# A two-block transformer on one core: the last block's bias rows made and stored during the third feed-forward part, and its scaled latents, their squares and rotation terms kept in PSUM

## The reference, cut to what matters

```python
# first block: h = h + 0.5*swiglu(..); a mixer (a scan in layer 0, sparse attention in layer 1); h = h + 0.5*swiglu(..)
# so there are four feed-forward parts, f0, f1, f2, f3; f3 is the last step of the first block
# second block:
xn = rms_norm_2(h, norm_mix_g)
qa, ka, va, c_q, c_kv, k_rope = split(xn @ w_in)        # widths 512 512 512 768 256 32
out_a = dilated_attention(rms(qa), rms(ka), va, rel_bias)     # 8 heads, logits + bias by distance
qb = rms_norm_2(c_q, cq_norm_g) @ w_uq                  # 8 heads of 96
kv = rms_norm_2(c_kv, ckv_norm_g) @ w_ukv               # 8 heads of 64 (key) + 64 (value)
qb, kb = rms_norm_2(qb, g), rms_norm_2([k_nope, k_rope for every head], g)
qb, kb = rotary embedding on the last 32 of 96 columns of each
out_b = causal_attention(qb, kb, vb)
h = h + concat(out_a, out_b) @ w_o
h = h + square(relu(rms_norm_2(h, norm_ffn_g) @ w_ff1)) @ w_ff2
```

## Time and profile before

| | us |
|---|---|
| median of 3 runs | 1781.03 (1777.22 to 1782.37) |
| the profiled execution, whole | 1785.45 |
| its span, first to last instruction | 1783.4 |
| TensorE busy, share of the span | 1612.4, 90% |
| GpSimd busy | 1097.2, 62% |
| VectorE busy | 801.8, 45% |
| ScalarE busy | 739.8, 41% |

### The profile page before, as it was taken

The page is one execution under the profiler, slowest core; times in us unless marked ns, Lnnn a source line. Parts: engine busy times, 40 slices in busy tenths (PEclk is TensorE's granted clock), DMA queues, the critical chain, the costliest instruction groups (busy, mean ns, idle before and its releaser), DMA issues.

```text
span 1783.4 us, 40019 instructions
## 1 busy us (share of the span) xinstructions
PE 1612.4 (90%) x15940; PEld 1522.0 (85%) x15940; DVE 801.8 (45%) x1576; ACT 739.8 (41%) x1204; POOL 1097.2 (62%) x552
## 2 busy tenths in 40 slices
PE   6999979659888899999999997999989969869998
PEld 6999979438886799999999985699989957769998
DVE  4332374684435733343334477663345635453300
ACT  4444434512312344444444432644435434544532
POOL 5778857343301578787787763068868753328896
PEclk9999989768767899999999997999999988889999
DMA  6454533100010344455444542035436632214552
GB/s 228 165 180 147 195 115 138 43 1 2 3 49 25 119 159 171 144 186 189 166 172 150 198 144 95 1 129 186 172 126 203 185 126 95 95 48 165 188 192 91
DMA packets 38777, 231.27 MB, mean 130 GB/s; under 512 B 4511, under 2 KB 7680, under 8 KB 17552
## 3 DMA queue, kind: packets, MB, share of 16 engines
q1 hardware_dynamic: 34560, 225.49, 35.9%
q10 hardware_dynamic: 4112, 4.31, 1.1%
HBM read 227.09 MB, written 2.62 MB: 129 GB/s over the span
## 4 chain that ended last, share of the span: by engine, by line
PE 77%; DVE 11%; issue 7%; POOL 3%; ACT 1%; DMA 0%; SPq 0%; DVEq 0%; ACTq 0%; POOLq 0%
PE PS L737 62%; POOL wlo L691 3%; PE PS L736 1%; DVE xl L1618 1%; DVE xg L1702 1%; DVE ss L1632 1%; PE PS L915 1%; PE PS L930 1%; PE PS L954 1%; PE PS L922 1%; DVE score L2038 1%; PE PS L960 1%; PE PS L1284 1%; ACT whi L2395 1%; DVE prnb L2316 1%
## 5 line engine op out<-in xcount | busy, mean ns | idle before, releaser
L691 POOL TENSOR_TENSOR wlo<-raw,whi 128x1024 fp32r<-128x1024 f32 (+1 forms) x472 | 1036.1, 2217 | 579.7 <-ACT whi L2395 530.2
L737 PE MATMUL PS<-xh,whi 128*128 128x272 f32 (+1 forms) x2336 | 689.5, 295 | 79.1 <-POOL wlo L691 35.9
L737 PE MATMUL PS<-xl,whi 128*128 128x272 f32 (+1 forms) x2336 | 678.5, 290 | 0.0
L737 PE MATMUL PS<-xh,wlo 128*128 128x272 f32 (+1 forms) x2336 | 677.3, 290 | 0.0
L2395 ACT ACTIVATE whi<-raw 128x1024 fp32r<-128x1024 f32 (+1 forms) x472 | 447.5, 980 | 260.0 <-PE PS L737 205.9
L737 PEld LDWEIGHTS PS<-xh,whi 128*128 128x128 f32 x2336 | 451.1, 193 | 93.4 <-issue 35.9
L737 PEld LDWEIGHTS PS<-xl,whi 128*128 128x128 f32 x2336 | 452.7, 194 | 0.6
L737 PEld LDWEIGHTS PS<-xh,wlo 128*128 128x128 f32 x2336 | 452.4, 194 | 0.0
L737 PE MATMUL PS<-hid_h,whi 128*128 128x272 f32 (+1 forms) x960 | 274.9, 286 | 12.1 <-POOL wlo L691 11.9
L737 PE MATMUL PS<-hid_h,wlo 128*128 128x272 f32 (+1 forms) x960 | 274.4, 286 | 0.0
L737 PE MATMUL PS<-hid_l,whi 128*128 128x272 f32 (+1 forms) x960 | 273.6, 285 | 0.0
(11 more groups left out here) (382 smaller groups left out, 1771.8 us busy)
## 6 DMA issues: line engine op xcount, KB each, us to landing
raw<-w_f_in_in SPq DMA_DIRECT2D x88, 1024.0 KB, 4.8
raw<-w_f_dn_in SPq DMA_DIRECT2D x64, 704.0 KB, 4.0
raw<-w_b_ff_in SPq DMA_DIRECT2D x32, 1024.0 KB, 4.8
raw<-w_rk_r_in SPq DMA_DIRECT2D x4, 1024.0 KB, 4.8
raw<-w_rk_k_in SPq DMA_DIRECT2D x4, 1024.0 KB, 4.7
raw<-w_rk_v_in SPq DMA_DIRECT2D x4, 1024.0 KB, 4.8
raw<-w_rk_o_in SPq DMA_DIRECT2D x4, 1024.0 KB, 4.9
raw<-w_at_q_in SPq DMA_DIRECT2D x4, 1024.0 KB, 5.0
```

What stands on the lines that cost most here:

```text
L691: nc.gpsimd.tensor_tensor(wlo[U % SPL][:, part], raw[U % RAW][:, part], whi[U % SPL][:, part].bitcast(F32), ALU.subtract).then_inc(s_lo, 1)
L737: mm(out, a, b, start=start and n == 0, stop=stop and n == 2, **kw)
```

## The change

1. The product of the bias rows moves from the head of the last block to the start of `f3_dn`, into the second bank of that stage's first group. VectorE's copy to `biasw` moves from after the normalization to right after the angle tables. ACT's store moves from behind `latent(0)` to right behind the two sines, ahead of `residual("f3_dn")`, whose first job is `hi` of unit 2.
2. The wait for the store and the eight bias loads move from behind the square of `kr` (just ahead of `hi(b_ka)`) to just ahead of `hi(b_cq+2)`.
3. The scaled latents (`cxf`) are now in PSUM banks 2 and 3, and their squares `csq` in bank 5.
4. `kg` is made from PSUM in one instruction instead of from `kr`; the key's product with the sine stays in PSUM bank 3, the queries' in bank 2; `qg` is made from PSUM before `qr` is drained, and its two instructions become one.

```diff
             def swiglu(f):
                 project(f + "_in", tok[f], 0, f, norm=f)
+                if f == "f3":
+                    G = G0["f3_dn"]
+                    pe.wait_ge(s_free, G - 1)
+                    pe.wait_ge(s_bc, 112)
+                    mm(PS[0:8, bank(G) + 1, 0:384], relb[:, :], distt[:, :], start=True, stop=True).then_inc(s_bwm, 1)
...
-            pe.wait_ge(s_bc, 112)
-            mm(PS[0:8, 4, 0:384], relb[:, :], distt[:, :], start=True, stop=True).then_inc(s_bwm, 1)
...
-            pe.wait_ge(b_kg, 1)
+            pe.wait_ge(s_free, G0["b_tail"] + 1)
             mm(PS[:, 3, 0:SEQ], rot_b[:, :], kg[:, :], start=True, stop=True).then_inc(s_hrot, 1)
...
+            dve.wait_ge(s_bwm, 1)
+            v.tensor_copy(biasw[:, :], PS[0:8, bank(G0["f3_dn"]) + 1, 0:384]).then_inc(s_bw, 1)
             residual("f3_dn", SEQ, 1, 2, 0.5, "b", VEC["norm_mix"], "b")
             rms("b", SEQ)
-            dve.wait_ge(s_bwm, 1)
-            v.tensor_copy(biasw[:, :], PS[0:8, 4, 0:384]).then_inc(s_bw, 1)
...
-                step.do(v.tensor_scalar(cxf[:, u % 2, 0, :], craw[:, u % 2, 0, :], col(VEC["cq_g"] + 2 * u), None, ALU.mult))
+                step.do(v.tensor_scalar(scaled_latent(u)[:, 0, :], craw[:, u % 2, 0, :], col(VEC["cq_g"] + 2 * u), None, ALU.mult))
...
-            v.tensor_tensor(kr[:, :], PS[:, G % 2, 0:SEQ], rstd[:, 0:SEQ], ALU.mult).then_inc(s_free, 1)
-            dve.wait_ge(s_free, G + 1)
-            v.tensor_scalar(kg[:, :], kr[:, :], col(VEC["kb_r"]), None, ALU.mult).then_inc(b_kg, 1)
+            step.do(v.tensor_tensor(kr[:, :], PS[:, G % 2, 0:SEQ], rstd[:, 0:SEQ], ALU.mult))
+            v.scalar_tensor_tensor(kg[:, :], PS[:, G % 2, 0:SEQ], col(VEC["kb_r"]), rstd[:, 0:SEQ], ALU.mult,
+                                   ALU.mult).then_inc(s_free, 1)
...
-            v.tensor_tensor(rtt[:, 0, :], PS[:, 3, 0:SEQ], cs_b[:, 1, :], ALU.mult).then_inc(b_rotd, 1)
+            step.do(v.tensor_tensor(PS[:, 3, 0:SEQ], PS[:, 3, 0:SEQ], cs_b[:, 1, :], ALU.mult))
             step(v.tensor_tensor(krot[:, :], kg[:, :], cs_b[:, 0, :], ALU.mult))
-            dve.wait_ge(b_rotd, 1)
-            step(v.tensor_tensor(krot[:, :], krot[:, :], rtt[:, 0, :], ALU.add))
+            v.tensor_tensor(krot[:, :], krot[:, :], PS[:, 3, 0:SEQ], ALU.add).then_inc(b_rotd, 1)
...
                 if J == 3:
+                    G = G0["b_uq"]
+                    dve.wait_ge(s_unit, 2 * (U0["b_uq"] + 1))
+                    v.tensor_scalar(qg[:, :, :], chunk_pair(G), col(VEC["qb_r"]), None, ALU.mult).then_inc(b_qg, 1)
                     queries_drain(0, qr[:, :, :])
-                    dve.wait_ge(s_free, G0["b_uq"] + 1)
-                    for q in range(2):
-                        v.tensor_scalar(qg[:, q, :], qr[:, q, :], col(VEC["qb_r"]), None, ALU.mult).then_inc(b_qg, 1)
...
@@ ACT
             for n in range(2):
                 act.wait_ge(s_ang, n + 1)
                 f(cs_b[:, n, :], cs_b[:, n, :], ACT.Sin).then_inc(s_sin, 1)
+            act.wait_ge(s_bw, 1)
+            act.dma_start(t["rows"].rearrange("(p h x) -> h p x", p=128, h=8),
+                          biasw[:, :].unsqueeze(1).broadcast_to([8, 128, 384])).then_inc(s_bst, 16)
             residual("f3_dn", SEQ, 1, 2, "b", "b")
...
             hi(U0["b_cq"] + 1)
             root("b", SEQ)
+            act.wait_ge(s_bst, 16)
+            pitch = 8 * 384 - 1
+            skewed = t["rows"][127:127 + 128 * pitch].rearrange("(p w) -> p w", w=pitch)
+            for hd in range(8):
+                act.dma_start(bias[:, hd, :], skewed[:, hd * 384:hd * 384 + 256]).then_inc(s_bld, 16)
             hi(U0["b_cq"] + 2)
             latent(0)
-            act.wait_ge(s_bw, 1)
-            act.dma_start(t["rows"].rearrange("(p h x) -> h p x", p=128, h=8),
-                          biasw[:, :].unsqueeze(1).broadcast_to([8, 128, 384])).then_inc(s_bst, 16)
             hi(U0["b_ckv"])
...
             f(krs[:, :], kr[0:32, :], ACT.Square).then_inc(b_sqk, 1)
-            act.wait_ge(s_bst, 16)
-            act.wait_ge(s_bst, 16)
...
-            for hd in range(8):
-                act.dma_start(bias[:, hd, :], skewed[:, hd * 384:hd * 384 + 256]).then_inc(s_bld, 16)
             hi(U0["b_ka"])
```

More of the change, by code:

```diff
@@ L411, in build @@
         craw = b2("craw", [128, 2, 2, SEQ])
-        cxf = b2("cxf", [128, 2, 2, SEQ])
-        csq = b2("csq", [128, 2, SEQ])
         squares = Region(rings)("squares", [128, 8, SEQ])
+        b2.here = rings + 4 * 8 * SEQ
         kr = b2("kr", [128, SEQ])
@@ L426, in build @@
         vbt = b2("vbt", [128, 2, 512])
-        rtt = b2("rtt", [128, 2, SEQ])
         hinva = b2("hinva", [16, SEQ])
@@ L551, in build @@
         b_sqk, b_sqq, b_sumk, b_sumq = sem("k_squared"), sem("q_squared"), sem("k_summed"), sem("q_summed")
-        b_kg, b_qg, b_rotd, b_f, b_om = (sem("k_rope_gain"), sem("q_rope_gain"), sem("rope_added"), sem("query_factor"),
+        b_qg, b_rotd, b_f, b_om = (sem("q_rope_gain"), sem("rope_added"), sem("query_factor"),
                                          sem("output_product"))
@@ L712, in build, with scaled_latent @@
         AT2, AT5 = 2, 5
+        def scaled_latent(g):
+            return PS[:, 2 + g % 2, :].rearrange("p (q n) -> p q n", q=2)
+        csq = PS[:, 5, :].rearrange("p (q n) -> p q n", q=2)
         def chunk_pair(G):
@@ L1549, in _ @@
             b_queries(1, 1)
-            pe.wait_ge(b_qg, 2)
+            pe.wait_ge(b_qg, 1)
             pe.wait_ge(s_hsc, AT5 + 7)
@@ L1569, in _ @@
             last.then_inc(b_sumq, 1)
-            pe.wait_ge(b_rotd, 3)
+            pe.wait_ge(b_rotd, 2)
             scores(8)
@@ L2184, in latent_low @@
                 dve.wait_ge(s_xh, X0["cq"] + g + 1)
-                low(latl[:, 2 * g:2 * g + 2, :], cxf[:, g % 2, :, :], lath[:, 2 * g:2 * g + 2, :], s_x)
+                low(latl[:, 2 * g:2 * g + 2, :], scaled_latent(g), lath[:, 2 * g:2 * g + 2, :], s_x)
             for u in range(4):
@@ L2194, in _ @@
                     dve.wait_ge(s_xh, X0["cq"] + u - 1)
-                step.do(v.tensor_scalar(cxf[:, u % 2, 0, :], craw[:, u % 2, 0, :], col(VEC["cq_g"] + 2 * u), None, ALU.mult))
-                v.tensor_scalar(cxf[:, u % 2, 1, :], craw[:, u % 2, 1, :], col(VEC["cq_g"] + 2 * u + 1), None,
+                step.do(v.tensor_scalar(scaled_latent(u)[:, 0, :], craw[:, u % 2, 0, :], col(VEC["cq_g"] + 2 * u), None, ALU.mult))
+                v.tensor_scalar(scaled_latent(u)[:, 1, :], craw[:, u % 2, 1, :], col(VEC["cq_g"] + 2 * u + 1), None,
                                 ALU.mult).then_inc(s_xm, 1)
@@ L2203, in _ @@
                         dve.wait_ge(s_css, 1)
-                    v.tensor_tensor(bt[0][:, :, :], bt[0][:, :, :], csq[:, :, :], ALU.add).then_inc(s_css, 1)
+                    v.tensor_tensor(bt[0][:, :, :], bt[0][:, :, :], csq, ALU.add).then_inc(s_css, 1)
             U, G = U0["b_tail"], G0["b_tail"]
@@ L2271, in _ @@
             dve.wait_ge(s_hb, AT5 + 5)
+            dve.wait_ge(b_rotd, 1)
             v.tensor_tensor(krf[:, :, :], krot[:, :].unsqueeze(1).broadcast_to([128, 2, SEQ]), spread_pair(2),
@@ L2350, in _ @@
                     dve.wait_ge(s_hrot, AT5 + 2)
-                    v.tensor_tensor(rtt[:, :, :], spread_pair(2), sin, ALU.mult).then_inc(b_rotd, 1)
+                    step.do(v.tensor_tensor(spread_pair(2), spread_pair(2), sin, ALU.mult))
                     dve.wait_ge(b_sqq, 1)
                     step(v.tensor_tensor(qr[:, :, :], qg[:, :, :], cos, ALU.mult))
-                    dve.wait_ge(b_rotd, 2)
-                    v.tensor_tensor(qr[:, :, :], qr[:, :, :], rtt[:, :, :], ALU.add).then_inc(b_rotd, 1)
+                    v.tensor_tensor(qr[:, :, :], qr[:, :, :], spread_pair(2), ALU.add).then_inc(b_rotd, 1)
                 if J == 7:
@@ L2682, in latent @@
                     act.wait_ge(s_css, 1)
-                f((bt[0], csq, csq, bt[1])[g][:, :, :], craw[:, g % 2, :, :], ACT.Square).then_inc(s_csq, 1)
+                f((bt[0][:, :, :], csq, csq, bt[1][:, :, :])[g], craw[:, g % 2, :, :], ACT.Square).then_inc(s_csq, 1)
                 act.wait_ge(s_xm, XM0["cq"] + g + 1)
-                f(lath[:, 2 * g:2 * g + 2, :], cxf[:, g % 2, :, :], ACT.Copy).then_inc(s_xh, 1)
+                f(lath[:, 2 * g:2 * g + 2, :], scaled_latent(g), ACT.Copy).then_inc(s_xh, 1)
             def heads_square(name, u, j):
@@ L2706, in _ @@
             f(krs[:, :], kr[0:32, :], ACT.Square).then_inc(b_sqk, 1)
-            act.wait_ge(s_bst, 16)
-            pitch = 8 * 384 - 1
-            skewed = t["rows"][127:127 + 128 * pitch].rearrange("(p w) -> p w", w=pitch)
-            for hd in range(8):
-                act.dma_start(bias[:, hd, :], skewed[:, hd * 384:hd * 384 + 256]).then_inc(s_bld, 16)
             hi(U0["b_ka"])
```

## The result

Over eight runs each, the changed kernel took 1772.08 us (1764.18 to 1777.35) and the kernel before 1781.57 (1775.86 to 1786.62): ratio 0.994, 95% interval 0.9915 to 0.9966, that is 6 to 15 us faster. (A ratio is always the time of a kernel divided by that of the kernel before.) The profiled execution took 1777.35, its span 1775.5. The forecast was 1769.2, range 1760 to 1779, and -11.8 as a difference; measured is -9.5.

The account below looks back on a forecast made before the run. Bound: TensorE's products plus holes, mainly its wait behind ScalarE's store. Terms -18.0 - 1.2 - 0.1 - 0.8 + 0.4 + 0.6 + 7.3 = -11.8, from the median 1781.0 to 1769.2 us; range 1760 to 1779.

Parts of the forecast that it names:

- Store out of the last block: Last block, before `b_ka`: TensorE's 15.1 us hole closes, and the slow first unit's 2.9 us with it; gain 18.0.
- VectorE's shorter path: Last block: scaled latents in PSUM shorten VectorE's path to `csq`, for which ScalarE and TensorE waited; gain 1.2.
- +0.4 for the loads: Bias loads ahead of `hi(b_cq+2)` hold ScalarE 3.7 us, delaying that unit's copy; cost 0.1 to 0.5, say 0.4.
- -0.1: Last block's head: the bias product and copy go away; gain 0 to 0.7, taken as 0.1.
- The head of f3_dn: Start of `f3_dn`: the copy to `biasw` and the store's issue delay `whi` of unit 2; cost 0.6.
- The store beside the loads: `f3_dn`: the store delays unit 6's load, giving TensorE a 5.6 us hole plus 1.7 restart; cost 7.3.
- The hidden store: Rival, `f3_dn`: unit 6's load waits only some 17 packets, landing at 1337.5, no hole; -19.1, 1762; chance 0.20.
- The second wait: Rival, last block: a slip of `b_ka` or `b_ukv` takes part of the gain, leaving -6, 1775; chance 0.16.
- The store that holds its engines to its end: Rival, `f3_dn`: unit 6 lands only with the store's end, hole 20.8 us; +4.6, 1786; chance 0.12.
- Operands in PSUM at J = 3: Attention step J = 3: `qg` takes about 0.8 instead of 2.75 us; gain 0 to 1.9, taken as 0.8.
- the probabilities meet the same POOL work: Attention step J = 3: probabilities behind the earlier logits still meet POOL's work, so the gain could be 0; no chance given.

Follow-up runs that it names:

- bias_only: Kernel before with only the bias product, copy, store and loads in their new places, all operands as they were: 1773.1 us, ratio 0.9946.
- copies32_late: Changed kernel with bias rows stored 32 times instead of 128, and bias product, copy, store and loads in their old places: 1765.0 us, ratio 0.9904.
- before_copies32: Kernel before with one edit, bias rows stored 32 times instead of 128 and loads of 32 partitions by four heads: 1765.6 us, ratio 0.9921.
- loads_back: Changed kernel with the wait and the eight bias loads back behind the square of `kr`: 1762.3 us in one execution.
- psum_only: Changed kernel with everything of the bias back in its old place, so only the operands in PSUM remain: 1783.3 us, ratio 1.000.
- copies64: Changed kernel with bias rows stored 64 times instead of 128, two heads to a load: 1764.9 us in one execution.
- copies32: Changed kernel with bias rows stored 32 times instead of 128, each load filling 32 partitions for four heads: 1763.9 us, ratio 0.990.
- after: The changed kernel itself, against the kernel before: 1772.08 us, ratio 0.994.
- after_again: The changed kernel measured once more, unaltered, against the kernel before: 1770.1 us, ratio 0.9946.

## Why the prediction was right, and where its numbers were off

**Store out of the last block, -18.0, and VectorE's shorter path, -1.2, +0.4 for the loads, -0.1.** Sum -18.9; the stage shows -19.4. `bias_only` gives the first with the loads' +0.4 in it as 73.3 - 55.2 = 18.1, `copies32_late` against `before_copies32` gives 1.3 for the second. The third does not show: with the loads back in their old place (`loads_back`) the stage takes 54.0, not less than 53.9. The two large terms hold, and their mechanism: ScalarE's wait was for the store, not for VectorE.

**The head of f3_dn, +0.6.** `whi` of unit 2 came 9.49 us after the first angle step, 8.89 before: 0.60.

**The store beside the loads, +7.3.** With the 0.6 this was 7.9; the stage shows 7.5. Unit 6's load landed at 1331.16 + 18.0 = 1349.2, 23.1 us after the store's issue; the forecast was 23.6. (In its sum the 0.7 for the smaller unit should be 0.9 by its own 2.9 us for 1024 KB; this changes nothing.) The hole was 4.6 us, forecast 5.6. The restart behind it was 1.5 (15 slow products in 3.2 us), forecast 1.7. What the forecast did not have is 0.7 at the stage's head, where the stretch at half the clock grew from 1.7 to 2.4 us; it also let TensorE come later to unit 6 and so shortened the new hole. 0.6 + 4.6 + 1.5 + 0.7 = 7.4. That the sum came within 0.4 is thus in part luck. That a load's delay could be carried over from `b_ka` with the store's issue as the origin was the choice on which the forecast hung. It held because the store had sent about as many packets in both places when the loads passed (71 to 76 an engine before, 74 after); the 57 of `psum_only` show that it need not have.

**The rivals.** The hidden store (a turn of 17 packets, landing at 1337.5) is out: 18.0 us instead of 8. The Trainium skill (DMA: Bandwidth & Descriptors, Queues, rings and completion order) has 64 descriptors as the ceiling of a turn. The 57 to 76 packets that each of the store's engines had sent before the loads passed are near that ceiling, in most runs somewhat above it, and far from its typical 9 to 17. No run shows the turn itself. The second wait is out: TensorE waits nowhere over 0.4 us between `b_cq` and `b_ukv`. The store that holds its engines to its end is what `copies64` and `copies32` show for up to 64 packets an engine, but with 128 the loads passed before the end, 23.1 us after the store's issue and not 36.6, which bounded the price.

**Operands in PSUM at J = 3, -0.8.** This is the term that did not come, and the timelines show where it went. In the kernel after, `qg` takes 0.75 us instead of 2.75, but now the next instruction of that size, the probabilities, runs beside GpSimd's low part. VectorE, and GpSimd's low part from 1494.66:

```profile
1493.88 0.75 DVE L2349 TENSOR_SCALAR qg<-PS,vec 128x512 f32<-128x512 f32 x1 [0.90 <-PE PS L740]
...
1495.76 2.75 DVE L2321 TENSOR_SCALAR prnb<-prb,binv 128x256 f32<-128x256 f32 x2
...
1498.92 0.42 DVE L2293 CUSTOM_DVE_ANT_0 lgb<-PS,bias 128x256 f32<-128x256 f32 x1 [0.21 <-PE PS L1427]
```

```profile
1494.66 3.69 POOL L689 TENSOR_TENSOR wlo<-raw,whi 128x1024 fp32r<-128x1024 f32 x2 [8.83 <-ACT whi L2399]
```

In the kernel before the same two probabilities took 1.02:

```profile
1506.57 1.02 DVE L2316 TENSOR_SCALAR prnb<-prb,binv 128x256 f32<-128x256 f32 x2
...
1507.71 0.41 DVE L2288 CUSTOM_DVE_ANT_0 lgb<-PS,bias 128x256 f32<-128x256 f32 x1
```

From VectorE's first instruction on the queries to these logits it is 5.15 us before and 5.04 after: the step gained 0.1. The prediction had named this rival (the probabilities meet the same POOL work) and still taken 0.8; this term is what it mis-sized.

The stretch became longer for another reason. From C to D the kernels with PSUM operands took 53.6 to 60.7 and those without 56.8 to 57.8, and the figures follow the granted clock: 1.00, 0.97, 0.94, 0.89 and 0.86 go with 53.6, 55.1, 56.6, 59.5 and 60.7. In the kernel after it was 0.89 against 0.91 before, +1.8 us where I had -0.8. Together with 0.9 us behind it, and less 0.9 in the two stages ahead, this is the difference between -11.8 and the -9.2 of the stages. At the same clock, 0.94, `loads_back` (56.6) and `bias_only` (56.8) differ by 0.2, and at 0.91 `psum_only` (58.1) and the kernel before (57.8) by 0.3 the other way, which agrees with the 0.1. What moves the clock is open. It is not the code of this stretch: `copies32` and the kernel after have the same code from C on, 53.6 against 59.6. It was not chance either between `after` and `after_again`.

## What to carry to other kernels

When a wait is moved away, look at what is waited for: here a store of 1536 KB of copies held the weight loads of bystanders as well as its own waiter, and a store a quarter as large closed the hole in either place. Do not price a transfer by its bytes: this store of 1536 KB took 36.6 us where a weight load of 1024 KB took 5.0, and sixteen engines instead of eight did not make it quicker. Take its rate from a row, and ask which loads need the same engines while it runs. Four load buffers gave some 9 us of slack here (a load 14 us late cost a hole of 4.6 us, and 1.5 for the restart). And when an instruction is made shorter, look whether the next one inherits its neighbour: the 2.0 us won on `qg` came back as 1.7 on the probabilities.

## What the runs showed of the hardware that I had not expected

- A DMA of 1024 pieces of 1536 bytes to memory took 36.6 us in the last block, 0.255 us a piece and engine while it ran. Cut in eight DMAs of one source partition each it took longer on twice the engines (19.5 packets a microsecond against 31), and ScalarE could issue only one in 6.8 us at the median.
- The stretch at half the clock behind an idle time has no fixed length. Behind the same wait of 6.8 us and the same code it lasted 3.7 us in the kernel before and 5.6 us in `psum_only`, which is 0.9 us of time.
- TensorE's granted clock can fall without an idle time before it. In the kernel after TensorE was busy without a break from 1427 to 1483 by the profile's count, and still:

```profile
1459.00:1465.00 6.00, 6.00 (x37) 5.11 (x36) 3.98 (x4) 1.28 (x2) 5.27 (x3) 1.00 0.35 108
1465.00:1471.00 6.00, 6.00 (x32) 5.68 (x32) 1.97 (x4) 1.38 (x2) 0.69 (x1) 0.72 0.17 71
1471.00:1477.00 6.00, 6.00 (x27) 4.75 (x26) 2.35 (x7) 1.41 (x5) 0.58 (x1) 0.59 0.52 175
```

In `copies32` the same products, in the same order, ran at 1.00 throughout:

```profile
1453.00:1459.00 6.00, 6.00 (x38) 4.97 (x38) 3.06 (x5) 1.91 (x2) 1.26 (x1) 1.00 0.15 64
1459.00:1465.00 6.00, 6.00 (x49) 5.42 (x50) 1.94 (x9) 2.32 (x9) 0.00 (x0) 1.00 0.47 175
```

This alone makes 6 us of a profile, as much as many edits.
